# A two-layer decoder trunk on one core: the order of the start and of the experts' evacuations is changed

## What is computed

```python
for l in range(2):
    h = x @ w_in[l]                      # 2726 columns: latents, FoX q/k/v + gate, dilated q/k/v
    mix = concat(latent attention 4 heads, forgetting attention 6, dilated attention 6) @ w_out[l]
    x = layer_norm(a * x + mix)
    x = layer_norm(a * x + cross_attention(x, mem[256, 1024], 4 heads))
    gates = router(x)                    # best group of four, then the best two of its experts
    ff = sum_e gates[:, e] * (silu(x @ w_gate[l, e]) * (x @ w_up[l, e])) @ w_down[l, e]   # 16 experts
    x = layer_norm(a * x + ff)
```

## Time and profile before

| | us |
|---|---|
| median of 3 runs | 922.77 (921.68 to 924.88) |
| the profiled execution | 923.28 |
| its span, first to last instruction | 921.7 |
| mean granted PE clock in it | 0.981 of 2.4 GHz |
| PE busy | 868.2 (94%) |
| DVE busy | 629.3 (68%) |
| ACT busy | 494.6 (54%) |
| POOL busy | 85.4 (9%) |

### The profile page before, as it was taken

One profiled execution on the slowest core, in us unless ns is written; L12 is line 12 of the kernel. 1 busy time (PEld: TensorE's weight loads), 2 busy tenths in 40 slices (PEclk: granted clock), 3 DMA queues, 4 the chain that ended last, 5 costly groups with the idle time before them and its releaser, 6 DMA issues.

```text
span 921.7 us, 12485 instructions
## 1 busy us (share of the span) xinstructions
PE 868.2 (94%) x4520; PEld 727.6 (79%) x4520; DVE 629.3 (68%) x1090; ACT 494.6 (54%) x793; POOL 85.4 (9%) x165
## 2 busy tenths in 40 slices
PE   5999999999999999999999999999999999999994
PEld 4987887779878777777789878868898787777773
DVE  6456765674556689989565567565654658989883
ACT  4545544444434577877355554444343456877761
POOL 7122200020010000000022140000100100000001
PEclk9999999999997999999999999999999999999997
DMA  9843342553333499999454434435534327999931
GB/s 302 278 127 114 138 138 92 197 202 112 110 108 121 153 346 344 361 351 335 148 168 138 143 114 138 138 117 181 186 115 142 110 92 257 359 354 342 364 103 47
DMA packets 124095, 177.08 MB, mean 192 GB/s; under 512 B 12304, under 2 KB 92704, under 8 KB 124032
## 3 DMA queue, kind: packets, MB, share of 16 engines
q1 hardware_dynamic: 122048, 169.56, 55.5%
q0 software_dynamic: 1984, 6.70, 2.4%
HBM read 175.18 MB, written 1.05 MB: 191 GB/s over the span
## 4 chain that ended last, share of the span: by engine, by line
PE 84%; DVE 8%; ACT 3%; issue 2%; POOL 2%; DMA 1%; DVEq 0%; ACTq 0%; POOLq 0%
PE bank L1465 22%; PE bank L1467 21%; PE bank L1466 21%; PE bank L1545 3%; DVE w_lo L527 3%; PE bank L1621 2%; PE bank L1727 2%; PE bank L1698 2%; PE bank L1601 2%; PE bank L1590 2%; PE bank L1579 2%; PE bank L1630 1%; PE bank L1568 1%; PE bank L1578 1%; ACT w_hi L521 1%
## 5 line engine op out<-in xcount | busy, mean ns | idle before, releaser
L527 DVE TENSOR_TENSOR w_lo<-raw,w_hi 128x1024 fp32r<-128x1024 f32 (+2 forms) x336 | 381.6, 1172 | 83.1 <-ACT w_hi L521 81.6
L521 ACT ACTIVATE w_hi<-raw 128x1024 fp32r<-128x1024 f32 (+2 forms) x336 | 326.3, 1007 | 121.5 <-PE bank L1467 120.9
L1465 PE MATMUL bank<-w_hi,xg_hi 128*128 128x512 f32 x256 | 104.6, 408 | 2.8 <-DVE w_lo L527 2.8
L1467 PE MATMUL bank<-w_hi,xg_lo 128*128 128x512 f32 x256 | 101.4, 396 | 0.0
L1466 PE MATMUL bank<-w_lo,xg_hi 128*128 128x512 f32 x256 | 101.3, 396 | 0.0
L1465 PE MATMUL bank<-w_hi,xT_hi 128*128 128x384 f32 (+2 forms) x256 | 87.2, 340 | 2.6 <-DVE xT_lo L1000 1.9
L1467 PE MATMUL bank<-w_hi,xT_lo 128*128 128x384 f32 (+2 forms) x256 | 85.2, 333 | 0.0
L1466 PE MATMUL bank<-w_lo,xT_hi 128*128 128x384 f32 (+2 forms) x256 | 85.0, 332 | 0.0
L626 POOL TENSOR_SCALAR st<-st 128x1 f32<-128x1 f32 x12 | 7.0, 580 | 684.5 <-ACT junk L768 683.9
L726 ACT ACTIVATE qkT<-bank 66x512 f32<-66x512 f32 (+2 forms) x32 | 19.0, 594 | 90.5 <-PE bank L1568 90.5
L1465 PE MATMUL bank<-w_hi,aT_hi 128*128 128x512 f32 x128 | 52.4, 409 | 8.3 <-DVE w_lo L527 6.0
(11 more groups left out here) (287 smaller groups left out, 1642.4 us busy)
## 6 DMA issues: line engine op xcount, KB each, us to landing
raw<-in_expert_w_gate_dram SPq DMA_DIRECT2D x128, 256.0 KB, 4.5
raw<-in_expert_w_up_dram SPq DMA_DIRECT2D x128, 256.0 KB, 5.3
raw<-in_expert_w_down_dram SPq DMA_DIRECT2D x64, 512.0 KB, 5.0
raw<-in_w_in_dram SPq DMA_DIRECT2D x48, 384.0 KB, 4.0
raw<-in_xattn_w_kv_dram SPq DMA_DIRECT2D x32, 512.0 KB, 3.6
raw<-in_w_mix_out_dram SPq DMA_DIRECT2D x16, 512.0 KB, 4.6
raw<-in_xattn_w_q_dram SPq DMA_DIRECT2D x16, 512.0 KB, 4.9
raw<-in_xattn_w_o_dram SPq DMA_DIRECT2D x16, 512.0 KB, 4.8
```

Of the source, the lines that this page charges most:

```text
L521: nc.scalar.activation(w_hi[:, split_slot(i, p), 0:w], raw[:, slot, 0:w], ACT.Copy).then_inc(hi_ready.sem, 1)
L527: nc.vector.tensor_tensor(w_lo[:, split_slot(i, p), 0:w], raw[:, slot, 0:w], w_hi[:, split_slot(i, p), 0:w].bitcast(F32), ALU.subtract).th ...
L1465: nc.tensor.matmul(o, lhs[0], rhs[0], start=first, stop=False, skip_group_check=shared)
L1467: return nc.tensor.matmul(o, lhs[1], rhs[0], start=False, stop=last, skip_group_check=shared)
```

## The change

**Start, layer 0 only.** SP issues the two tiles of tokens first, each with a semaphore of its own, then the positions; the memory tokens follow behind sub 3. POOL makes the identity first, then the frequencies, then issues the small transfers of layer 0 (two gains, forget bias) and the router's bias, then the other constants. The dilated masks move behind the copies of the rotary key (L661), ahead of the rotation of DQ; DVE waits for them (`const_pool` 56) ahead of its evacuation of the first pair of heads. PE waits only for the identity and the tokens. Its filler products ahead of the projection are left out in layer 0, and it turns the memory between subs 3 and 4. ACT's sines stand between hi(0) and hi(1), DVE's constants between lo(3) and lo(4), and both evacuate the memory behind sub 7. The scratch of the angles is laid elsewhere.

**Experts, both layers.** The order within a turn is new, and y comes ahead of aT; the waits of PE for y are one for each half.

```diff
 @@ sync
+            for t in range(TT):
+                sp.dma_start(xs[:, t, :], x[0][t * P:(t + 1) * P, :]).then_inc(x_in[t], 16)
             sp.dma_start(pos_i[:, :], positions[0].rearrange("(t p) -> p t", p=P), ...
-            sp.dma_start(mem_tok[:, :, :], mem[0].rearrange("(t p) d -> p t d", p=P)).then_inc(mem_in, 16)
-            sp.dma_start(xs[:, :, :], x[0].rearrange("(t p) d -> p t d", p=P)).then_inc(start_in, 16)
...
                     load(l, i, i % RAW, straight(l, i))
+                    if l == 0 and i == index["A", 3]:
+                        sp.dma_start(mem_tok[:, :, :], mem[0].rearrange("(t p) d -> p t d", p=P)).then_inc(mem_in, 16)
 @@ gpsimd
-            pool.dma_start(rbias[:, :], ...).then_inc(bias_in, 16)
+            nc.gpsimd.memset(ident[:, :], 0.0).then_inc(ident_in, 1)
+            pool.wait_ge(ident_in, 1)
+            nc.gpsimd.affine_select(out=ident[:, :], ...).then_inc(ident_in, 1)
             for i in range(32):
                 nc.gpsimd.memset(freq[:, :, i:i + 1], float(inv[i])).then_inc(const_pool, 1)
+            small(0)        # gains of q and kv, b_forget: three transfers
+            pool.dma_start(rbias[:, :], ...).then_inc(bias_in, 16)
...
-            step(...)       # the dilated masks
+            def dilated_masks(): ...
-            pool.wait_ge(const_a, 2)
-            pool.wait_ge(tables, 1)
             for l in range(L):
                 norm(l, 0, ln_mix_g, ln_mix_b)
+                if l:
+                    small(l)
...
+                if l == 0:
+                    pool.wait_ge(const_a, 2)
                 rotate(l, kr, kr, 1, 16, 2, 0)
...
+                if l == 0:
+                    dilated_masks()
                 for n, (name, q) in enumerate((("DQ", dq), ("DK", dk))):
 @@ scalar
             def expert_turn(l, e, par, first, p=None, base=0, y=None):
-                split_hi(act, l, first, p)
-                split_hi(act, l, first + 1, p)
+                for j in range(3):
+                    split_hi(act, l, first + j, p)
                 silu_of(l, par, base - 2)
-                split_hi(act, l, first + 2, p)
                 split_hi(act, l, first + 3, p)
-                aT_of(l, e, par)
                 if y is not None:
                     y_of(l, y, base)
                 split_hi(act, l, first + 4, p)
+                aT_of(l, e, par)
                 split_hi(act, l, first + 5, p)
...
                 split_hi(act, l, 0)
+                if l == 0:
+                    sines()
                 split_hi(act, l, 1)
...
+                silu_of(l, 1, NSUB - 4)
                 split_hi(act, l, NSUB - 2)
                 split_hi(act, l, NSUB - 1)
-                silu_of(l, 1, NSUB - 4)
                 aT_of(l, NE - 1, 1)
 @@ vector: expert_turn in the same new order (lo, act for hi, silu)
+                act_of(l, NE - 1, 1)
                 split_lo(dve, l, NSUB - 2)
+                aT_of(l, NE - 1, 1)
                 split_lo(dve, l, NSUB - 1)
-                act_of(l, NE - 1, 1)
-                aT_of(l, NE - 1, 1)
                 y_of(l, NG - 1)
...
                     if s >= 3 and (s - 3) % 2 == 1:
+                        if l == 0 and s == 4:
+                            dve.wait_ge(const_pool, 56)
                         evac_o(l, s - 3)
 @@ tensor
-            pe.wait_ge(const_pool, 45)
-            pe.wait_ge(fp_tables, 3)
-            ...             # memory transposes
-            pe.wait_ge(start_in, 16)
+            pe.wait_ge(ident_in, 2)
...
-                if p is not None and first:
-                    pe.wait_ge(y_v.sem, y_v.at(l, p * 2 + 2))
                 for c_ in range(2):
                     parts = sub_in(l, i + c_, p)
                     for h in range(2):
+                        if p is not None and first and c_ == 0:
+                            pe.wait_ge(y_v.sem, y_v.at(l, p * 2 + h + 1))
...
+                if l == 0:
+                    pe.wait_ge(x_in[0], 16)
                 turn_x(l, "XT0", 0, -1)
...
-                if not l:
-                    pe.wait_ge(mem_v, 4)
-                keep_busy(11)
+                if l:
+                    keep_busy(11)
...
-                for i in range(0, 8):
+                for i in range(0, 4):
                     gemm(l, i)
+                if l == 0:
+                    turn_memory()
+                for i in range(4, 8):
+                    gemm(l, i)
+                if l == 0:
+                    pe.wait_ge(fp_tables, 3)
+                    pe.wait_ge(mem_v, 4)
...
                 turn_a(l, NE - 1, 1)
+                pe.wait_ge(selT_a.sem, selT_a.at(l, 2))
+                scatter(l, 0, range(NG - 1))      # tile 0, groups 0 to 2
                 experts_down(l, NE - 1, NSUB - 2, 1, False, True)
-                for g in range(NG):
-                    scatter(l, g)
+                scatter(l, 1, range(NG - 1))
+                scatter(l, 0, [NG - 1])
+                scatter(l, 1, [NG - 1])
```

More of the change, by code:

```diff
@@ L382, in build @@
         ov_y_in = signal("ov_y_in", 1 + 2 * EPG)
-        start_in = sem("start_in")
+        x_in = [sem(f"x_in{t}") for t in range(TT)]
+        ident_in = sem("ident_in")
         warmed = sem("warmed")
@@ L581, in _ @@
[L581 to L592, removed]
@@ L692, in _, with sines, turn_memory @@
         def _(act):
-            act.wait_ge(angles, 1)
-            nc.scalar.activation(sinb[:, :, :].rearrange("p t d -> p (t d)"), ang[:, 6, :], ACT.Sin).then_inc(const_a, 1)
-            nc.scalar.activation(cosb[:, :, :].rearrange("p t d -> p (t d)"), ang[:, 7, :], ACT.Sin).then_inc(const_a, 1)
-            for n in range(4):
-                act.wait_ge(mem_done, n + 1)
-                t, h = n // 2, n % 2
-                nc.scalar.activation(memT_hi[:, 4 * h:4 * h + 4, t * P:(t + 1) * P],
-                                     bank[4 + n][:, :].rearrange("p (k m) -> p k m", k=4), ACT.Copy).then_inc(mem_a, 1)
+            def sines():
+                act.wait_ge(angles, 1)
+                nc.scalar.activation(sinb[:, :, :].rearrange("p t d -> p (t d)"), ang[:, 6, :], ACT.Sin).then_inc(const_a, 1)
+                nc.scalar.activation(cosb[:, :, :].rearrange("p t d -> p (t d)"), ang[:, 7, :], ACT.Sin).then_inc(const_a, 1)
+            def turn_memory():
+                for n in range(4):
+                    act.wait_ge(mem_done, n + 1)
+                    t, h = n // 2, n % 2
+                    nc.scalar.activation(memT_hi[:, 4 * h:4 * h + 4, t * P:(t + 1) * P],
+                                         bank[4 + n][:, :].rearrange("p (k m) -> p k m", k=4), ACT.Copy).then_inc(mem_a, 1)
             def wait_job(l, name):
@@ L908, in _ @@
                                                  bank[XG_BANKS[f % 3][n]][:, :], ACT.Copy).then_inc(xg_a.sem, 1)
-                for i in range(N1 + 4, N1 + 6):
+                for i in range(N1 + 4, N1 + 7):
                     split_hi(act, l, i)
@@ L915, in _ @@
                 silu_of(l, 0, N1 + 4)
-                for i in range(N1 + 6, N1 + 8):
+                for i in range(N1 + 7, N1 + 9):
                     split_hi(act, l, i)
                 aT_of(l, 0, 0)
-                for i in range(N1 + 8, N1 + 10):
-                    split_hi(act, l, i)
+                split_hi(act, l, N1 + 9)
                 for p in range(TURNS):
@@ L1271, in expert_turn @@
             def expert_turn(l, e, par, first, p=None, y=None):
-                split_lo(dve, l, first, p)
-                split_lo(dve, l, first + 1, p)
+                for j in range(3):
+                    split_lo(dve, l, first + j, p)
                 act_of(l, e, par)
-                split_lo(dve, l, first + 2, p)
                 split_lo(dve, l, first + 3, p)
-                aT_of(l, e, par)
                 if y is not None:
@@ L1717, in turn_sel, with scatter @@
                 ins.then_inc(selT_done.sem, 1)
-            def scatter(l, g):
-                if g == 0:
-                    pe.wait_ge(selT_a.sem, selT_a.at(l, 2))
-                for h in range(2):
-                    pe.wait_ge(y_v.sem, y_v.at(l, 2 * g + h + 1))
-                    for t in range(TT):
+            def scatter(l, t, groups):
+                for g in groups:
+                    for h in range(2):
+                        pe.wait_ge(y_v.sem, y_v.at(l, 2 * g + h + 1))
                         for v in (y_hi, y_lo):
```

131 lines of the change are left out of this document (77 added, 54 removed).

## The result

The changed kernel takes 907.82 us (median; 906.73 to 908.64), the kernel before 922.88 in the same comparison (921.68 to 924.88): a ratio of 0.9834 [0.9814, 0.9854]. I had forecast 913.0 us and a range of 909 to 918, so the sign was right and the size wrong: 15.1 us were gained, and the sum had 10.0. The profiled execution took 908.64 us, its span is 906.9.

The account below looks back on a forecast made before the run. TensorE, busy 94% of the span, was taken as the bound, so only its waits could be won: 5.8 (y turns) + 3.3 (layer ends) + 0.9 (start) = 10.0 us, giving 913.0 us, range 909 to 918.

Parts of the forecast that it names:

- The y turn: Expert turn that also evacuates a group's sum: the 1.00 us gap ahead of its down projection goes, 5.8 us over 6.
- TensorE's own 8.73 us bind: Expert turns: 36 products and the transposes make 8.73 us, TensorE's own pace, nothing else late once the gap goes.
- rival D: Every expert turn: aT's low half comes too late behind the fifth half; at 0.5 us missed, 928 us; 4%.
- The layer's end: Last expert and scatter of each layer: gaps of 0.70 and 0.93 us both go, 1.63 per layer, 3.3 in all.
- Weight stream: Experts' sub loads, issued 12 slots ahead, stay hidden; without this cover 2.9 us per layer would be lost to landings.
- rival C: Experts: VectorE takes TensorE's place as the bound, half of each y gap stays; 915.8 us, or 917; 8%.
- The start: Layer 0 ahead of the experts: 5.1 - 2.2 - 1.74 - 0.2 = 0.9 us gained; ends 2.3 gained, 5.3 lost.
- the clock: Start of layer 0: idle TensorE runs its first products at 1.2 GHz, costing 1.5 to 2.9 us, taken as 2.2.
- The 5.1: Start of layer 0: the first product comes 5.1 us earlier, at 15.1 instead of 20.16; between 1.8 and 5.5.
- A: Start gives nothing back or costs: 9.1 gained at the experts, 0 to 5.3 lost ahead; about 916.5 us; 17%.
- B: Clock isn't low: full clock at the first product, or the low stretch behind the gates falls away; 910.3 us; 10%.
- E: Experts: reordered layer end and y turns each bring another low clock stretch, costing 12 us; 925 us; 1%.

Follow-up runs that it names:

- y_first: The kernel before with the evacuation of y moved ahead of aT in the experts' turns, nothing else; 917.51 us, ratio 0.9923.
- y_and_a: The kernel before with y ahead of aT and aT also behind the fifth half in the experts' turns; 908.32 us, ratio 0.9817.
- pool_late: The changed kernel with GpSimd's layer 0 transfers, gb too, issued only when weight sub 3 has landed; 905.65 us, ratio 0.9823.
- x_first: The changed kernel with token evacuations ahead of everything and angles, sines and constants behind block 3; 903.86 us, ratio 0.9789.
- x_pool_filled: The changed kernel with tokens evacuated first, GpSimd's transfers behind block 3 and 16 filler transposes; 899.56 us, ratio 0.9751.
- third_first: The kernel before with only the third weight half moved ahead of the silu in the experts' turns; 925.67 us, ratio 1.0021.
- tail_only: The kernel before with only the layer's last expert and scatter in the changed order; 921.50 us, ratio 0.9973.
- experts_only: The kernel before with the experts' part of the change alone, the start as it was; 906.02 us, ratio 0.9791.
- start_only: The kernel before with the start's part of the change alone, the experts as they were; 925.26 us, ratio 1.0013.

## Why the prediction was wrong

**The y turn: mechanism right, term mis-sized.** "I take 0.97 per y turn (1.00 less a 0.03 restart)". In the whole change it was 1.24 (9.71 to 8.46). The bracket understates a wait: the product before the gap is drawn 0.39 long where the next could start after 0.23, so 1.00 idle is 1.16 lost, and the restart costs 0.08 more (0.31 instead of 0.23 to the next product) rather than giving 0.03. With `y_first` the y turn went from 9.71 to 8.73; the other 0.27 is the hidden wait that remained. 6 x 1.24 = 7.5, not 5.8.

**The step that failed: "36 products at 0.227 (34.94/154) and the transposes make 8.73 us ... TensorE's own 8.73 us bind".** 36 x 0.227 is 8.17, which leaves 0.56 for two transposes; after the change they take 0.14 (375.07 to 375.21) and the product behind them 0.08 more than its usual distance. Most of the rest was a wait in each ordinary turn. `y_first` against `y_and_a` shows it: 9.2 us between them, with only aT's place changed (26 turns at 0.27 are 7.0, the turns into the last one 2 x 0.86 = 1.7; what shortened those beyond the 0.27 I haven't followed). Of the 9.2, 20 ordinary turns x 0.27 = 5.5 us are what the sum counted as nothing. It is rival D with the opposite sign: I asked only whether aT would be late behind the fifth half, not whether the fifth half was late behind aT. The trace has that low half's end at 397.95, where TensorE could have gone on at 397.91 (397.68 + 0.23) and went on at 398.09.

**The layer's end: mechanism right, term mis-sized.** 1.63 forecast, 2.13 measured alone (0.88 + 1.25): the brackets 0.70 and 0.93, each short by 0.16 and the second by the restart too, make 2.03; 0.10 stays unexplained. In the whole change a layer's end gained 2.40, the hidden wait of turn 14 (0.27) among it. 4.8 us, not 3.3.

**Weight stream, VectorE (rival C).** As forecast: no turn waits for a landing, and VectorE, busy 34.58 of 36 us, holds nobody up.

**The start: the sum failed in one term.** Measured, between the two profiled executions: 2.6 - 1.5 - 1.75 - 0.2 = -0.85, against 5.1 - 2.2 - 1.74 - 0.2. Transposes (1.75) and the latent chain (0.34 of issue instead of 0.14) came as forecast, the clock cost less than I took. The 5.1 failed, by the sentence "Small transfers issued by GpSimd near 3 to 5.5 us bring their standstill into the weight landings of blocks 1 to 3, wanted from 11 us on: nothing". It gave a cost without a row for it, and it counted only the four small ones: the 1 MB of `gb` that the change moved from 17.88 to 7.80 stands nowhere in the sum. With all six moved away sub 1 lands at 9.40 and the first product is at 15.44, against my 15.1; with them sub 1 lands at 12.86 and the first product is at 17.56. How the 2.1 us are shared between the small ones and `gb` stays open, as no run moves one without the other. The table load wasn't hidden either: ScalarE's idle time of 8 to 9.8 was gone, since sub 0 landed at 9.21 instead of 7 and the load began at 10.15. With the landings put right it stands in the chain, 9.16 to 10.46, and the load is followed by the sine 0.02 later. So the page of the Trainium skill that I cited (ScalarE: Activation LUTs, "What ACT_TABLE_LOAD costs"), 2.66 us with its drain, isn't borne out by these rows: in the kernel after, the Copy ended at 10.14 (9.23 + 0.91) and the sine began at 11.45, 1.31 us for the whole switch.

**Rivals.** A's mechanism was there (the start gives nothing back: 0.9 lost in this pair, inside its 0 to 5.3), but its time wasn't, since the experts brought 17.7 for its 9.1. B fell in both forms: the clock was low at the start, and the low stretch behind the gates is there in both layers as before (3.4 us). C, D and E fell: turns of 8.46 us leave no room for a loss in them. Of the signs named for being wrong (a turn over 8.8, a first product after 18, a mask holding VectorE) none came, though the forecast was off: all three looked for losses, and the miss was a gain.

**What the range left out.** It bounded unknown costs, and took the known part, TensorE's own pace, as exact. The 17.7 us at the experts are 8.6 over the forecast: 5.5 in ordinary turns, 1.7 in y turns, 1.5 at the ends (rounded). The start's miss of 1.8 went the other way, and so did the scatter between the layers and 0.3 us ahead of the experts: 10.0 + 8.6 - 1.8 - 1.8 - 0.3 = 14.7. So the total came nearer to the forecast than its terms did, by luck.

## What to carry to other kernels

Before an engine's pace is taken from busy time over instructions, compare starts: multiply the shortest distance of two products by their number, and ask the missing time of each stretch for a wait, since drawn ends overlap and hide up to 0.16 us each time. Where two engines share the preparation of operands in written-out orders, put what needs nothing from the bottleneck's last step ahead of what does; the same move fixed the rare wait (y) and the common one (fifth half). At a start, count every transfer that any queue issues within the landing time of the first operands, also those that a removed wait lets go early, and check the gain several product blocks later: here order alone brought 6.2 us at the first product and kept 1.8, while order, landings and clock together brought 6.2 and kept 7.7.

## What the runs showed of the hardware

- Small transfers of GpSimd, 3 to 128 KB, took 6 to 9 us to land beside the weight stream. Together with 1 MB of `gb` from the same engine they pushed 416 KB subs from 1.2 us apart (`pool_late`) to 2.6 to 3.8; the two were not taken apart.
- TensorE's low stretch at the start ended at 20.79 with the change and at 20.44 with the first product 2.1 us earlier. In `x_first` it was 10.89 to 14.31. With 84 transposes in the idle time, and with 16 in `x_pool_filled`, the clock was 1.00 from 10 to 20 us. One profiled execution each.
- A drawn end hides a wait: products start 0.23 us apart and are drawn 0.39 long, and the distance behind a wait is 0.31. A wait of 0.26 us showed no idle time at all.
- The kernel before has a low stretch at its start in some executions: `third_first`, `tail_only`, `y_first` and `y_and_a`, whose start is the same, show one (below, `third_first`), the profiles of before and of `experts_only` none. Their first heads are at 60.05 to 60.24, the other two at 58.64 and 58.58, so 1.4 to 1.7 us of a start's time is decided by the execution profiled. The change's 59.48 lies between the two groups: 0.9 later than the profile of before, 0.6 to 0.8 earlier than four of the others. That its start gains nothing therefore rests on the ten times of `start_only`, and the 0.9 on this pair of profiles alone.
```profile
19.80:23.20 3.40, 3.01 (x9) 2.88 (x10) 1.95 (x3) 0.00 (x0) 1.07 (x4) 0.50 1.06 384
```
